# Gate stage of an encoder block: the sums of the seven products are begun in PSUM from ScalarE's copies

## The reference

```python
h = rmsnorm(x, norm2_g)
x = x + (jax.nn.silu(h @ w_gate) * (h @ w_up)) @ w_down     # 1024 -> 2816 -> 1024
return rmsnorm(x, normf_g)
```

## Time and profile before

| | |
|---|---|
| median of 3 runs | 2484.71 us (2484.14 to 2484.93) |
| profiled execution, its own time | 2485.58 us |
| its span in the profile | 2483.8 us |
| TensorE busy | 2464.0 us, 99% |
| VectorE busy | 1682.5 us, 68% |
| ScalarE busy | 937.1 us, 38% |
| gate stage, in the span | about 582 to 1850 us |

### The profile page before, as it was taken

The page is one execution under the profiler, slowest core; times in us unless marked ns, Lnnn a source line. Parts: engine busy times, 40 slices in busy tenths (PEclk is TensorE's granted clock), DMA queues, the critical chain, the costliest instruction groups (busy, mean ns, idle before and its releaser), DMA issues.

```text
span 2483.8 us, 31712 instructions
## 1 busy us (share of the span) xinstructions
PE 2464.0 (99%) x11029; PEld 2038.3 (82%) x11029; DVE 1682.5 (68%) x2578; ACT 937.1 (38%) x1718; POOL 167.1 (7%) x222
## 2 busy tenths in 40 slices
PE   9999999999999999999999999999999999999998
PEld 7888878887888888888888888888888888888887
DVE  5655877899767767867677686676774464455665
ACT  5534466546333333433333333333332232233333
POOL 2555400000000000000000000000000000000000
PEclk9999999999999999999999999999999999999999
DMA  6432766787323223523232432222256654354554
GB/s 185 112 88 89 229 214 246 258 266 269 125 83 124 110 80 119 191 109 110 88 118 110 163 142 96 99 110 97 110 193 215 245 194 169 123 191 142 203 190 149
DMA packets 174776, 382.05 MB, mean 154 GB/s; under 512 B 13576, under 2 KB 74856, under 8 KB 165476
## 3 DMA queue, kind: packets, MB, share of 16 engines
q1 hardware_dynamic: 166016, 350.83, 41.4%
q0 software_dynamic: 8240, 29.94, 3.2%
q10 hardware_dynamic: 432, 0.14, 0.0%
HBM read 254.24 MB, written 126.62 MB: 153 GB/s over the span
## 4 chain that ended last, share of the span: by engine, by line
PE 86%; DVE 1%; DMA 1%; issue 0%; ACT 0%; ACTq 0%
PE bank L352 28%; PE bank L354 28%; PE bank L353 28%; DMA a_raw<-ha_scr 1%; PE bank L2090 0%; DVE a_lo L2684 0%; PE bank L1377 0%; PE bank L1063 0%; DVE scratch L1037 0%; DVE zy_late L1048 0%; DVE w_lo L2707 0%; DVE uv_lo L1075 0%; ACT a_hi L2492 0%; DVE wm_lo L1289 0%; DVE scratch L1040 0%
## 5 line engine op out<-in xcount | busy, mean ns | idle before, releaser
L352 PE MATMUL bank<-a_hi,w_hi 128*128 128x512 f32 x1848 | 720.4, 390 | 6.6 <-DVE a_lo L2684 3.2
L354 PE MATMUL bank<-a_hi,w_lo 128*128 128x512 f32 x1848 | 719.5, 389 | 0.0
L353 PE MATMUL bank<-a_lo,w_hi 128*128 128x512 f32 x1672 | 651.0, 389 | 0.0
L352 PEld LDWEIGHTS bank<-a_hi,w_hi 128*128 128x128 f32 x1848 | 347.3, 188 | 81.1 <-issue 4.9
L354 PEld LDWEIGHTS bank<-a_hi,w_lo 128*128 128x128 f32 x1848 | 347.2, 188 | 72.2
L353 PEld LDWEIGHTS bank<-a_lo,w_hi 128*128 128x128 f32 x1672 | 314.3, 188 | 64.8
L352 PE MATMUL bank<-t_hi,s_hi 128*128 128x512 f32 x924 | 359.5, 389 | 0.0
L354 PE MATMUL bank<-t_hi,s_lo 128*128 128x512 f32 x924 | 359.5, 389 | 0.0
L353 PE MATMUL bank<-t_lo,s_hi 128*128 128x512 f32 x924 | 359.5, 389 | 0.0
L2505 ACT ACTIVATE w_hi<-t_raw 128x512 fp32r<-128x512 f32 x256 | 162.0, 633 | 461.9 <-PE bank L354 379.1
L2859 DVE TENSOR_TENSOR s_lo<-s_raw,s_hi 128x512 fp32r<-128x512 f32 x231 | 155.9, 685 | 230.8 <-ACT s_hi L2580 230.8
(11 more groups left out here) (284 smaller groups left out, 3212.4 us busy)
## 6 DMA issues: line engine op xcount, KB each, us to landing
s_scr<-sums_out SPq DMA_DIRECT2D x33, 1792.0 KB, 5.9
s_raw<-s_scr SPq DMA_DIRECT2D x42, 1024.0 KB, 5.0
w_raw<-in_w_gate SPq DMA_DIRECT2D x64, 512.0 KB, 3.5
w_raw<-in_w_up SPq DMA_DIRECT2D x64, 512.0 KB, 4.4
wd_staged<-in_w_down SPq DMA_DIRECT2D x121, 256.0 KB
a_raw<-ha_scr SPq DMA_DIRECT2D x21, 1024.0 KB, 4.9
s_raw<-s_scr SPq DMA_DIRECT2D x21, 768.0 KB, 5.0
x<-in_x SPq DMA_DIRECT2D x24, 512.0 KB, 5.6
```

The source lines that it names most:

```text
L352: pe.matmul(out, w_hi, m_hi, start=first, stop=False, **checks)
L353: pe.matmul(out, w_hi, m_lo, start=False, stop=False, **checks)
L354: return pe.matmul(out, w_lo, m_hi, start=False, stop=last, **checks)
```

## The change

Bank b6 is no longer cleared by product 2: ScalarE copies bank a into it after product 0 (`begin_sum`), and product 2 adds to that. After product 2 ScalarE copies b6 into bank d (where products 4 and 6 then add) and into `c12` in SBUF (`begin_up`, two copies). Bank c after product 1 is copied to `p5` in SBUF (`keep_product`). VectorE's `u_sums` and `gate_of_odd` are gone; silu of the odd half reads bank d. VectorE keeps `up_of_odd` (bank d plus `p5`), the sum into `c12` and the two multiplications. TensorE now waits for `begin_sum` ahead of product 2 and for the first copy of `begin_up` ahead of product 4; before, it waited for `p1`'s copy ahead of product 3. The four transposes that share a bank in the output projection set the start flag only at the first of them.

```diff
 (ScalarE, order at the first tile of all)
         feed.round_w(0, 0, 0, 2)
+        feed.begin_sum(0, 0)
         act.wait_ge(pair_ready, product_of(LAST, 4))
         feed.round_a(0, 2)
...
         squares(NT - 1, 3, 2 * NT)
+        feed.keep_product(0, 0)
         feed.round_a(0, 3)
         root(LAST + 2, slice(3, 4))
         scaled(LAST + 1, 2)
-        feed.copy_first()
+        feed.begin_up(0, 0)
         feed.round_a(0, 4)
...
+        def begin_sum(n, e):
+            act.wait_ge(p_ready, n * 7 + 1)
...
+            act.activation(bank[e][1][:, :], bank[e][0][:, :], ACT.Copy).then_inc(copied, 1)
...
+        def keep_product(n, e):
+            act.wait_ge(p_ready, n * 7 + 2)
...
+            act.activation(held(n)[0][:, :], bank[e][2][:, :], ACT.Copy).then_inc(copied, 1)
...
+        def begin_up(n, e):
+            act.wait_ge(p_ready, n * 7 + 3)
...
+            act.activation(bank[e][3][:, :], bank[e][1][:, :], ACT.Copy).then_inc(copied, 1)
...
+            act.activation(c12[:, :], bank[e][1][:, :], ACT.Copy).then_inc(copied, 1)
 (ScalarE, tile)
-            act.activation(p1[:, :], bank[e][0][:, :], ACT.Copy).then_inc(p1_done, 1)
+            begin_sum(n, e)
             if more:
                 round_w(*follow, 0)
...
+            keep_product(n, e)
+            if more:
+                round_w(*follow, 1)
+            begin_up(n, e)
+            if more:
+                round_w(*follow, 2)
             if turn:
                 round_a(b + 1, 0)
                 round_a(b + 1, 1)
...
 (VectorE, tile)
             if begins:
-                u_sums(n, e)
                 rest_of_a(b, 5)
                 rest_of_a(b, 6)
-                up_of_odd(n, e)
             make_t(*follow, 0)
             make_t(*follow, 1)
...
             rest_of_w(*follow, 3)
-            if not begins:
-                up_of_odd(n, e)
+            up_of_odd(n, e)
...
-            gate_of_odd(n, e)
             rest_of_w(*follow, 6)
             odd_done(n, b, i, e)
 (TensorE, tile)
             ready(2)
-            product(b6, 2, b).then_inc(p_ready, 1)
+            pe.wait_ge(copied, n * 4 + 1)
+            product(b6, 2, b, more=True).then_inc(p_ready, 1)
             ready(3)
-            pe.wait_ge(p1_done, n + 1)
             product(a, 3, b, more=True).then_inc(p_ready, 1)
             ready(4)
-            if not early:
-                pe.wait_ge(c_done, n * 7 + (6 - 14))
-            product(d, 4, b).then_inc(p_ready, 1)
+            pe.wait_ge(copied, n * 4 + 3)
+            product(d, 4, b, more=True).then_inc(p_ready, 1)
             ready(5)
-            pe.wait_ge(c_done, n * 7 + 2)
             product(c, 5, b, more=True).then_inc(p_ready, 1)
             ready(6)
-            pe.wait_ge(c_done, n * 7 + 3)
+            pe.wait_ge(c_done, n * 4 + 1)
             product(d, 6, b, more=True).then_inc(p_ready, 1)
```

More of the change, by code:

```diff
@@ L54 @@
 Programs = namedtuple("Programs", "sync gpsimd scalar vector tensor")
-ActFeed = namedtuple("ActFeed", "round_a round_w copy_first silu_first second_tile rest")
-DveFeed = namedtuple("DveFeed", "make_t rest_of_a rest_of_w u_sums up_of_odd second_tile rest")
+ActFeed = namedtuple("ActFeed", "round_a round_w begin_sum keep_product begin_up silu_first second_tile rest")
+DveFeed = namedtuple("DveFeed", "make_t rest_of_a rest_of_w up_of_odd second_tile rest")
 SpFeed = namedtuple("SpFeed", "first_weights second_weights rest")
@@ L2089, in transposes @@
                     d = 4 * k + i
-                    mm = pe.transpose(t_ps[2 * tile + k][:, i, :], xn[:, tile, d * P:(d + 1) * P], eye[:, :])
+                    mm = pe.matmul(t_ps[2 * tile + k][:, i, :], xn[:, tile, d * P:(d + 1) * P], eye[:, :], start=i == 0,
+                                   stop=i == 3, is_transpose=True, skip_group_check=True)
                 mm.then_inc(transposed, 1)
@@ L2283, in tile_of, with first_two @@
         return i * 2 + (FT * b + e)
+    def first_two(n):
+        return isinstance(n, int) and n < 2
     def set_of(b, i, e):
@@ new lines, in gate_of_even, with gate_of_odd @@
+        def gate_of_even(n, e):
+            act.wait_ge(p_ready, n * 7 + 4)
+            if not fixed(n, 0):
+                act.wait_ge(c_done, n * 4 + (3 - 4))
+            act.activation(silu[:, 0, :], bank[e][0][:, :], ACT.Silu).then_inc(silu_done, 1)
+        def gate_of_odd(n, e):
+            act.wait_ge(p_ready, n * 7 + 7)
+            if not fixed(n, 0):
+                act.wait_ge(c_done, n * 4)
+            act.activation(silu[:, 1, :], bank[e][3][:, :], ACT.Silu).then_inc(silu_done, 1)
@@ L2507, in tile @@
         def tile(b, i, e, more, turn):
-            n = tile_of(b, i, e)
+            n = 1 if fixed(i, 0) and b == 0 else tile_of(b, i, e)
             follow = (b, i, 1) if e == 0 else (b, i + 1, 0)
[L2511 to L2514, removed]
-            act.activation(p1[:, :], bank[e][0][:, :], ACT.Copy).then_inc(p1_done, 1)
+            begin_sum(n, e)
             if more:
@@ L2524, in tile @@
                 round_a(b + 1, 1)
[L2525 to L2528, removed]
+            gate_of_even(n, e)
             if more:
@@ L2676, in down @@
             act.activation(half, half, ACT.Copy, scale=rstd[:, one:one + 1]).then_inc(out_ready, 1)
-        return ActFeed(round_a, round_w, copy_first, silu_first, second_tile, rest)
+        return ActFeed(round_a, round_w, begin_sum, keep_product, begin_up, silu_first, second_tile, rest)
     def vector(dve):
@@ L2751, in even_done @@
             dve.tensor_tensor(dst, c12[:, :], silu[:, 0, :], ALU.mult).then_inc(c_done, 1)
-        def gate_of_odd(n, e):
-            p1, _, _ = held(n)
-            dve.wait_ge(p_ready, n * 7 + 7)
-            dve.tensor_tensor(c21[:, :], bank[e][3][:, :], p1[:, :], ALU.add).then_inc(c_done, 1)
         def odd_done(n, b, i, e):
-            _, _, c22 = held(n)
+            _, c22 = held(n)
             dve.wait_ge(silu_done, n * 2 + 2)
@@ L2907, in down @@
             rest_of_s(1)
-            u_sums(n, 1)
             rest_of_t(2)
@@ L2915, in down @@
             rest_of_t(4)
-            gate_of_odd(n, 1)
             odd_done(n, b, i, 1)
@@ L2989, in down @@
             last_norm(3)
-        return DveFeed(make_t, rest_of_a, rest_of_w, u_sums, up_of_odd, second_tile, rest)
+        return DveFeed(make_t, rest_of_a, rest_of_w, up_of_odd, second_tile, rest)
     def tensor(pe):
@@ L3060, in first_tile @@
             ready(2)
-            product(b6, 2, 0).then_inc(p_ready, 1)
+            pe.wait_ge(copied, 1)
+            product(b6, 2, 0, more=True).then_inc(p_ready, 1)
             transposes_even()
             ready(3)
-            pe.wait_ge(p1_done, 1)
             product(a, 3, 0, more=True).then_inc(p_ready, 1)
@@ L3067, in first_tile @@
             ready(4)
-            pe.wait_ge(ahead.x1_ready, 2 * NT)
-            product(d, 4, 0).then_inc(p_ready, 1)
+            pe.wait_ge(copied, 3)
+            product(d, 4, 0, more=True).then_inc(p_ready, 1)
             ready(5)
-            pe.wait_ge(c_done, 2)
             product(c, 5, 0, more=True).then_inc(p_ready, 1)
             ready(6)
-            pe.wait_ge(c_done, 3)
+            pe.wait_ge(c_done, 1)
             product(d, 6, 0, more=True).then_inc(p_ready, 1)
```

88 lines of the change are left out of this document (36 added, 52 removed).

## The result

The changed kernel takes 2498.04 us (median of 5 runs, 2497.24 to 2500.79) beside 2484.93 us for the kernel before (5 runs, 2484.14 to 2487.61): ratio 1.0054, 95% interval 1.0043 to 1.0065, or 13.1 us slower. The forecast was 2497.7 us, 13.0 us slower. The profiled execution took 2497.24 us, span 2495.4, and is the fastest of the five.

What follows compares the result with a forecast made beforehand. TensorE, busy 99% of the span, was taken to bound the kernel. Losses of 3.8 (first tile), 4.4 and 4.8 us (turns), 13.0 in all, added to the 2484.71 us median gave 2497.7 us; 8-in-10 range 2491 to 2503.

Steps and rivals of the forecast that it cites:

- Operations, inner tile: In inner tiles, VectorE's savings and ScalarE's copies run beside TensorE, each awaited copy with 1.9 us to spare: 0 us.
- First turn, (1): At the first turn, two `begin_up` copies ahead of `round_a` 0 take 0.96 us of queue; product 6 waits 0.43 us.
- First turn, (2): At the first turn, `begin_sum` stands behind `round_a` 6, which waits for load 6; product 2 starts 3.29 us late.
- First turn, (3) and (4): `begin_up` waits behind `round_w` 1 and VectorE's `make_t` 0; product 4 starts 4.4 us late, both earlier delays included.
- Second turn: Same chain, other slack: product 6 loses 0.44 us, product 2 is about 3.3 us late, product 4 4.8 us late.
- First tile of all: `begin_sum` delays `round_a` 2 by 0.74 us; `begin_up` waits for product 2, `round_a` 4 3.6 to 3.9 later; product 5 loses 3.8.
- TensorE's clock: After new idle stretches the clock may halve: taken as 0, with 1.4 us for each of three places as other end.
- Sum: First tile and both turns, 3.8 + 4.4 + 4.8 = 13.0 us, all of it reaching the end.
- The turns are covered: Rival, 8%: copies at the turns come in time, only the first tile's 3.8 us stay: 2488.5 us.
- The clock falls at each new gap: Rival, 17%: slow products at the turns and first tile aren't absorbed, 13.0 + 3 x 1.4 = 17.2 us: 2501.9 us.
- Every tile pays: Rival, 5%: slower copies use up inner tiles' 1.9 us, then each 0.1 us costs 6.6 us: 2504 us or more.
- VectorE's relief pays: Rival, 2%: TensorE's waits for `a_lo`, `w_lo` and `p`, 6.6 us, vanish and nothing new comes: 2478.1 us.

Runs made afterwards that it cites:

- the first tile's edit: Changed kernel with `round_a` 4, the second `scaled` and `round_w` 4 ahead of `begin_up` in the first tile of all: 2496.77 us, 1.0046 of the kernel before.
- seven operations: Changed kernel with three more VectorE additions in each of the 54 inner tiles, into spare tiles: 2500.42 us, 1.006 of the kernel before.
- five copies: Changed kernel with `begin_up`'s copy into bank d made five times in each of the 54 inner tiles: 2541.90 us, 1.0227 of the kernel before.
- all orders: Changed kernel with `begin_sum`, `begin_up` and `up_of_odd` moved at the turns and ScalarE's first tile reordered: 2485.14 us, 0.9997 of the kernel before.
- the three copies: Changed kernel with `begin_up`'s copy into bank d made three times in each of the 54 inner tiles: 2499.80 us, 1.0059 of the kernel before.

## Why the prediction was right, point by point

- **Operations, inner tile: 0.** Shown from three sides: no wait in the window, 1.23 us more for free and 2.45 us at a price (slack 1.8 us, foretold 1.9), and VectorE's three operations put back with no wait in it. A bank-to-bank copy takes 0.58 us here too.
- **First turn, (1).** 0.96 us of copies: measured 0.97; product 6 is 0.47 us late, foretold 0.43.
- **First turn, (2).** Product 2 starts at 1021.06 - 2.22 = 1018.84, 3.31 us after it was due, foretold 3.29. One slip: I wrote that the profile would show a wait of 3.2 us. It shows 2.56, since 0.47 of the lateness had been spent at product 6 and 0.12 in that product behind its wait, and since the profile counts idle time from the modelled end of a matmul, here 0.16 us behind the time at which the next was due.
- **First turn, (3) and (4).** Taking off 2.22 us, `round_w` 1 is at 1024.78, the copy at 1025.32, product 4 at 1026.05; foretold 1024.8, 1025.3, 1026.0. Lost 4.42 us, foretold 4.4.
- **Second turn.** 0.46 + 4.38 = 4.84, foretold 4.8; product 2 is 3.15 us late, foretold 3.3. That both turns come to the same 18.21 us, though they differed by 0.43 before, says that one chain (the rest of slices 4 to 6, `make_t` 0, `round_w` 1, the copy) now sets both.
- **First tile of all.** 3.87 us, foretold 3.8; product 2 0.65 us later, foretold 0.7; `round_a` 4 3.91 us later, foretold 3.6 to 3.9. The queue behind `begin_up` was read rightly. That the size fits to 0.1 us is luck: in the six other kernels with these instructions the tile lost 4.4 to 5.0 us, because the slow clock reached further, and the prediction's upper end for it was 4.7.
- **TensorE's clock.** It fell at both turns, and product 4's wait took it up, as forecast; two products of 4.42 us are 3.4 us of TensorE's 5.4 us more of busy time (1 to 4 us was foretold; the rest lies mostly in the first tile, which is 3.87 us longer with only 2.2 us more idle time ahead of products 2 and 5). This was the step with the least behind it, and the experiments say why it held. In the kernel with the first tile's edit the clock did not fall at the first turn; product 2 took 2.84 us and product 4 waited, TensorE in that kernel:

```profile
1021.64 0.47 PE L352 MATMUL bank<-a_hi,w_hi 128*128 128x512 f32 x1 [2.37 <-ACT bank L2516]
...
1029.03 0.47 PE L352 MATMUL bank<-a_hi,w_hi 128*128 128x512 f32 x1 [1.67 <-ACT bank L2532]
```

  and product 6 to product 4 was 18.21 us all the same. So it was at two more turns where the clock did not fall (first turn with seven operations, second turn with five copies: product 2 took 2.84 and 2.82 us, product 4 waited 1.76 and 1.64). With the clock slow, or full, the end is the same where a later wait is the binding one; in the kernel with `begin_sum` alone moved it wasn't, and the clock cost 1.6 us at each turn.
- **Sum.** 13.0 us foretold, 13.1 by the times, 13.3 by the trace. The interval of the times is 10.7 to 16.2 us, so agreement to 0.1 us is luck; that the trace has each of the three places where the prediction had it is not.
- **Rivals.** *The turns are covered*: no, they lose 9.4 us, though they can be covered by moving `begin_sum`, `begin_up` and `up_of_odd`. *The clock falls at each new gap*: at the turns it fell for nothing. In the first tile it cost nothing new in the changed kernel's trace, and 0.5 to 1.2 us more in the six others, so there the rival is right in part. *Every tile pays*: none does, and the price it named, 0.1 us a tile from 1.9 us on, is that of the kernel with five copies. *VectorE's relief pays*: no.

The larger errors of size are those of experiments. One is the gain of the first tile's edit (2.2, not 3.3 us), for which I left out `begin_sum` and the second copy. Another is `begin_sum` alone (17.0, not 12.6), for which I left out the clock, as I did in the first tile with all orders (28.27 us, not 27). What decides whether the clock falls in a given execution stays open.

## What to carry to other kernels

Where one engine is busy 99% of the time, an edit that takes 130 us of work from another is worth what the first engine's waits say, here nothing; what it costs is read at the few places where the queue order differs from the inner loop's: the first tile and each change of block. A copy that is wanted one product earlier must also stand one product earlier in its engine's queue, and what it stands behind (a rounding that waits for a transfer, a sum that waits for three slices of another engine) sets its time, not its own 0.58 us. Waits in series share one chain: follow it to the last of them before moving the first.

## What the runs showed that I had not expected

- Product 6 to product 4 was 18.21 us to within 0.02 in 13 of the 14 turns of seven kernels (the changed one, the first tile's edit, each copy alone, the three copies, the five, the seven operations), at either clock; the fourteenth was the one with the slow loads. In twelve of the thirteen product 4 starts right behind `begin_up`'s copy, as the chain has it. The thirteenth, the second turn with `begin_up` moved alone, has another cause, TensorE's own slow product 2, and the same number by chance.
- The length of the idle time does not tell whether the clock falls. Ahead of product 2 at a turn it fell after 2.18 and 2.21 us, and three times, after 2.31, 2.37 and 2.42 us, it did not. Ahead of product 5 in the first tile it fell after 1.78 us (first tile's edit) and did not after 2.52 us (changed kernel). The Trainium skill ("TensorE: Matmul & The Clock Gate", Part 1: The HAM clock gate) says that how many matmuls run slow varies from run to run of one kernel; the traces agree as far as they can, each being of another kernel: product 2 at the first turn took 4.42 us in the changed kernel and 2.84 with the first tile's edit, and the two have the same instructions there.
- The same loads took 4.8 us to landing in one execution and 7.2 in another (median of seven transfers of 1 MB). With the slow clock that lasted longer there, this moved a turn by 2.8 us without an edit.
